# FFN 2's down-projection in seven products instead of eight

## The chip, the cores and the metric

The kernel runs on one core of one Trainium2 chip. The metric is the device time of one execution in microseconds (us). Before the change the median of three runs is 3400.17 us (3399.27 to 3403.31).

## What is computed

One inference step of a decoder layer over 1056 tokens (1024 of a prompt, 32 of samples), D_MODEL 1024, D_FF 2816. Only the last part matters here:

```python
def swiglu(x, w_in, w_out):
    gate, up = jnp.split(x @ w_in, 2, axis=-1)
    return (jax.nn.silu(gate) * up) @ w_out

y = h + 0.5 * rmsnorm(swiglu(rmsnorm(h, ffn2_pre), ffn2_w_in, ffn2_w_out), ffn2_post)
```

All values are float32. The kernel splits each operand of a matmul into a high and a low half (a cast to fp32r, and the difference to the value) and adds three matmuls: high by high, high by low, low by high. A tile of weights or of hidden values therefore costs a load, a cast on ScalarE and a subtraction on VectorE before TensorE can use it.

## The kernel before

Both FFNs are built by `ffn_units`; FFN 2 is called from `outputs_ffn`. Each engine has an in-order queue, written out by hand, and semaphores say when an operation may start. `sync`, `scalar`, `vector`, `gpsimd` and `tensor` are the queues of SP (which issues all loads and stores here), ScalarE, VectorE, POOL and TensorE; each calls `during(h, k)` at its step, by which `outputs_ffn` puts its own work (norms, turned rows, stores) between the steps.

The up-projection ends with hidden row tiles t = 0 to 21 of 128 features by 1056 tokens. It already uses seven products in place of eight (`product`, L2887), with weight sums on POOL (L2829 to L2834). Each finished row tile is stored to DRAM as `d_hid` (`store_h`, L2510).

The down-projection (`out_step`, L2897) multiplies `w_out` (22 tiles of 128 features by 1024) with the hidden values. Tokens are in chunks (`SPANS`): 0 to 383, 384 to 767, and the last 288. For each chunk there are two passes, one for each half of the output features: h = 0 to 5. In a pass, at every k of 22, one unit of weights u = 22 h + k (128 x 512) meets hidden tile k, in 4 output blocks by 3 matmuls: 12 matmuls. Sums stay in four PSUM banks, and the passes alternate between banks 0 to 3 and 4 to 7.

A unit is loaded to one of eight raw slots (`load_unit`, L2560), cast (`unit_high`, L2568) to one of four slots, and its low half made (`unit_low`, L2572). The cast of u + 3 waits until TensorE is through with u - 1. Hidden tiles come back from `d_hid` one at a time (`load_hid`, L2584; `hid_high`, L2594; `hid_low`, L2600) through a ring of four. POOL has only sums of squares here (`sum_pool`, L2981). After a chunk's two passes come `square` (L2966), `copy_out` (L2974, L2972), the mean (`sum_y`), `root_y`, `norm` (L3010), the residual sum (L3981), transposes of rows (L4120), copies of these (L3849) and stores; the last chunk has its residual transposed early (L4141, copied by L3853) and ends the kernel with L4145, L4151 and L4006.

Of the kernel before, what the change touches and what calls it, by code (L numbers as in the profile page):

```python
# [2348 lines left out]
def ffn_units(nc, m, sem, w_in, w_out, d_hid, first_hi, first_lo, x, t_val, t_hi, t_lo, pair_mem, hid_hi, hid_lo, gb, rstd, pre, spans, acc, staged):  # L2349
# [18 lines left out]
    e.y_normed, e.h_resid = sem("y_normed"), sem("h_resid")  # L2368
    win = w_in.rearrange("o (f p) n -> p (o f) n", p=P)
# [232 lines left out]

    EARLY = {2: range(0, 3), 3: range(3, 6), 4: range(6, 8), 5: range(8, 10)}
    BEFORE = 10

    def sync(sp, before_odd, during):
        load_pair(sp, 2)
# [38 lines left out]
    def scalar(act, t_free, during):  # L2646
# [6 lines left out]
        for t in range(2, FT):  # L2653
# [8 lines left out]
            for i in range(7):  # L2662
                if s + 6 + i < N1:
                    pair_high(act, s + 6 + i)
                elif i in (3, 4, 5):
                    unit_high(act, i - 3)
                if t == FT - 1 and i in EARLY:
                    for n in EARLY[i]:
                        hid_high(act, n)
                if i in (4, 6):  # L2670
                    a = (i - 4) // 2
                    act.wait_ge(e.gate_done, 6 + 2 * (t - 2) + a + 1)
                    nc.scalar.activation(silu[:, halves(a)], silu[:, halves(a)], ACT.Silu).then_inc(e.silu_done, 1)
        for h in range(6):
# [50 lines left out]
    def vector(dve, scale_in, between, during):  # L2725
# [14 lines left out]
        for t in range(2, FT):  # L2740
# [5 lines left out]
            def next_low(i):  # L2746
                if s + 6 + i < N1:
                    pair_low(dve, s + 6 + i)
                elif i in (3, 4, 5):
                    unit_low(dve, i - 3)  # L2750
                if t == FT - 1 and i in EARLY:
# [46 lines left out]
        pair_h(dve, FT - 1, 1)  # L2798
        for h in range(6):
# [17 lines left out]
    def gpsimd(pool, x_dead):  # L2817
        t_differences(pool)
        x_dead()
        for t in range(2, FT):  # L2820
# [14 lines left out]
            if t == 2:  # L2835
                t_low_pool(pool)

# [63 lines left out]
    def tensor(pe, during, bank_free):  # L2901
# [10 lines left out]
        for t in range(2, FT):  # L2912
            for i in range(7):
                product(pe, t, i)
        for h in range(6):
# [27 lines left out]
    def result(j):  # L2943
        c, o = divmod(j, KT)
        lo, hi = spans[c]
        return m.ps[:, o, 0:hi - lo], acc[:, o, 0:hi - lo]
# [10 lines left out]
    def square(act, j):  # L2957
        c, o = divmod(j, KT)
        act.wait_ge(e.out_mm, output_done(j))
# [6 lines left out]
        nc.scalar.activation(ring(c, o) if o else total(c), result(j)[0], ACT.Square).then_inc(e.y_squared, 1)  # L2966
# [9 lines left out]
    def sum_pool(pool, c):  # L2976
        for o in range(1, 8 if c < 2 else 4):
# [5 lines left out]
    def sum_y(pe, c, bank):  # L2983
        lo, hi = spans[c]
        mean = m.cst[:, C_MEAN:C_MEAN + P]
        if c < 2:
            pe.wait_ge(e.y_copied, KT * c + bank + 1)
# [17 lines left out]
    def norm(dve, c, f, post):  # L3005
        y = result(KT * c + f)[1]
        if f == 0:
            dve.wait_ge(e.y_rooted, c + 1)
            dve.wait_ge(e.y_copied, KT * c + KT)
# [6 lines left out]
    e.total, e.ring, e.last_gain = total, ring, None  # L3016
# [518 lines left out]
def outputs_ffn(nc, m, keep, w_a, w_b, w_o, gates, ob_dram, d_resid, d_hid, w_in, w_out, y_prompt, y_sample):  # L3535
# [8 lines left out]
    with ExitStack() as ctx:  # L3544
# [32 lines left out]
        pair_mem, acc = m.pair_mem, m.acc_chunk  # L3577
# [9 lines left out]
        def staged_hid(c, k):  # L3587
# [5 lines left out]
                      SPANS, acc, staged_hid)  # L3593
# [11 lines left out]
        def pair(i):  # L3605
            return (6, 4, 6, 6, 4, 6, 2, 4, 6)[i]
# [6 lines left out]
        def row_out(i):  # L3613
            n = P if i < TT else NS
            return row_of(i)[0:n, :].rearrange("p (b f) -> p b f", b=2), m.ps[0:n, pair(i):pair(i) + 2, :]
# [23 lines left out]
        def _(sp):  # L3639
# [55 lines left out]
            def res_load(c):  # L3695
                lo, hi = SPANS[c]
                if c == 0:
                    sp.wait_ge(e.y_copied, 1)
# [15 lines left out]
            def during(h, k):  # L3714
                if h in (1, 3) and k == 6:
                    res_load(h // 2)
                elif h == 3 and k == 8:
                    sp.dma_start(res_last, d_resid[:, :, 6 * P:T]).then_inc(res_in_last, 16)
                elif h in (3, 5) and k in (0, 1, 2):
                    store_row(3 * (h // 2 - 1) + k)  # L3720
# [7 lines left out]
        def _(act):  # L3728
# [117 lines left out]
            def row(i):  # L3846
                dst, src = row_out(i)
                act.wait_ge(turned, i + 1)
                nc.scalar.copy(dst, src).then_inc(row_act, 1)  # L3849

            def res_row(t):
                act.wait_ge(res_mm, t + 1)
                nc.scalar.copy(row_of(6 + t).rearrange("p (b f) -> p b f", b=2), m.ps[:, 6:8, :]).then_inc(res_moved, 1)  # L3853

            def during(h, k):
                if h == 4 and k in (8, 10, 12):
                    res_row((k - 8) // 2)
                if h in (2, 4):
                    if k == 6:
                        e.root_y(act, h // 2 - 1, 4)  # L3860
                    elif k in (18, 19):
                        row(3 * (h // 2 - 1) + k - 18)
                    elif k == 21:
                        row(3 * (h // 2 - 1) + 2)
# [447 lines left out]
```

## Time and profile before

| | us |
|---|---|
| median of three runs | 3400.17 |
| the profiled execution's span | 3400.1 |
| TensorE busy | 3305.8 (97%) |
| VectorE busy | 1871.2 (55%) |
| ScalarE busy | 1456.3 (43%) |
| POOL busy | 700.0 (21%) |
| HBM read and written | 309.92 MB, 75.57 MB |

The span is that of the one execution that was profiled. A busy share is an average over stages with different limits; the change touches about the last 290 us, so the rows below are mostly of that stretch. The granted TensorE clock is given as a share of full speed: 1.00 is 2.4 GHz.

### The profile page before, as it was taken

Reading aid. Unit: us, or ns where it says so; the run is one execution under the profiler, and the core shown is the slowest. Engines: PE = TensorE matmul, PEld = TensorE weight load, DVE = VectorE, ACT = ScalarE, POOL = GpSimd, SP = SyncE. Lnnn points to the kernel's source line nnn. Section 1 sums busy time; section 2 is a strip of 40 time slices with the busy share of each in tenths; the row PEclk is TensorE's granted clock in tenths of the full one; section 3 lists DMA queues with packets and bytes.
Section 4 is the critical chain, followed back from the end, with each engine's and each line's share of the span. In section 5 each row is a group of like instructions: output and inputs, shape, how many; then the busy total and the mean of one; then the engine's idle time right before and its main releaser. Section 6 shows DMA issues by size and latency. Waiting matters only on the chain. (4 is left out here: it accounts for less than half of the span.)

```text
span 3400.1 us, 70872 instructions
## 1 busy us (share of the span) xinstructions
PE 3305.8 (97%) x28190; PEld 3137.6 (92%) x28190; DVE 1871.2 (55%) x3334; ACT 1456.3 (43%) x3056; POOL 700.0 (21%) x651
## 2 busy tenths in 40 slices
PE   7999999998999999999999999999999899999999
PEld 7999999997888888877899999998999899999998
DVE  6655565764555555554455555554441855556555
ACT  5222234555555455443344444444323722223444
POOL 3323310112222222100022222222001332221000
PEclk9999999999999999999999999999999999999999
DMA  4222237742222222379511122224532322224664
GB/s 167 76 79 79 87 109 230 221 135 81 70 70 70 71 70 70 109 254 369 188 47 56 58 59 59 59 59 136 165 88 70 123 86 76 76 76 151 200 207 132
DMA packets 353606, 390.03 MB, mean 115 GB/s; under 512 B 22792, under 2 KB 259416, under 8 KB 353134
## 3 DMA queue, kind: packets, MB, share of 16 engines
q1 hardware_dynamic: 343126, 352.18, 33.1%
q0 software_dynamic: 10080, 33.05, 2.7%
q8 instruction: 228, 3.74, 0.5%
q14 instruction: 88, 0.72, 0.1%
q10 hardware_dynamic: 84, 0.35, 0.0%
HBM read 309.92 MB, written 75.57 MB: 113 GB/s over the span
## 5 line engine op out<-in xcount | busy, mean ns | idle before, releaser
L673 PE MATMUL ps<-p_hi,w_hi 128*128 128x352 f32 x912 | 305.6, 335 | 1.8 <-PEq L123 1.4
L673 PE MATMUL ps<-p_hi,w_lo 128*128 128x352 f32 x912 | 294.5, 323 | 0.0
L673 PE MATMUL ps<-p_lo,w_hi 128*128 128x352 f32 x912 | 294.0, 322 | 0.0
L2062 PE MATMUL ps<-p_hi,w_hi 128*128 128x352 f32 x840 | 291.0, 346 | 2.7 <-PEq L123 1.4
L2062 PE MATMUL ps<-p_hi,w_lo 128*128 128x352 f32 x840 | 277.2, 330 | 0.0
L2062 PE MATMUL ps<-p_lo,w_hi 128*128 128x352 f32 x840 | 277.2, 330 | 0.0
L673 PEld LDWEIGHTS ps<-p_hi,w_hi 128*128 128x128 f32 x912 | 173.1, 190 | 4.2 <-issue 2.7
L2897 PE MATMUL ps<-op_hid_hi,w_hi 128*128 128x384 f32 (+1 forms) x528 | 171.5, 325 | 3.7 <-DVE w_lo L2572 2.0
L673 PEld LDWEIGHTS ps<-p_lo,w_hi 128*128 128x128 f32 x912 | 173.2, 190 | 0.0
L2897 PE MATMUL ps<-f_hid_hi,w_hi 128*128 128x352 f32 x528 | 171.5, 325 | 1.6 <-DVE w_lo L2572 1.6
L673 PEld LDWEIGHTS ps<-p_hi,w_lo 128*128 128x128 f32 x912 | 172.2, 189 | 0.0
L2897 PE MATMUL ps<-f_hid_lo,w_hi 128*128 128x352 f32 x528 | 170.0, 322 | 0.0
L2897 PE MATMUL ps<-f_hid_hi,w_lo 128*128 128x352 f32 x528 | 169.9, 322 | 0.0
L2897 PE MATMUL ps<-op_hid_hi,w_lo 128*128 128x384 f32 (+1 forms) x528 | 169.6, 321 | 0.0
L2897 PE MATMUL ps<-op_hid_lo,w_hi 128*128 128x384 f32 (+1 forms) x528 | 169.6, 321 | 0.0
L2062 PEld LDWEIGHTS ps<-p_hi,w_hi 128*128 128x128 f32 x840 | 160.5, 191 | 8.2 <-issue 3.1
L2062 PEld LDWEIGHTS ps<-p_lo,w_hi 128*128 128x128 f32 x840 | 160.9, 192 | 0.2
L2062 PEld LDWEIGHTS ps<-p_hi,w_lo 128*128 128x128 f32 x840 | 160.5, 191 | 0.0
L2572 DVE TENSOR_TENSOR w_lo<-w_raw,w_hi 128x512 fp32r<-128x512 f32 x136 | 100.5, 746 | 83.2 <-ACT w_hi L2568 82.8
L414 ACT ACTIVATE at_prob<-ps,at_nmax 128x256 f32<-128x256 f32 (+7 forms) x128 | 94.2, 737 | 82.4 <-DVE at_nmax L520 80.7
L2568 ACT CAST w_hi<-w_raw 128x512 fp32r<-128x512 f32 x136 | 83.8, 620 | 100.5 <-PE ps L2897 100.1
L347 ACT ACTIVATE at_rotx<-ps 32x352 f32<-32x352 f32 x192 | 87.4, 455 | 88.6 <-DVE at_cosx L468 54.7
(707 smaller groups left out, 10374.4 us busy)
## 6 DMA issues: line engine op xcount, KB each, us to landing
w_raw<-in_ffn_w_out_dram SPq DMA_DIRECT2D x136, 256.0 KB, 3.4
w_raw<-in_w_in_dram SPq DMA_DIRECT2D x67, 512.0 KB, 4.2
sa_v<-in_cache_v_dram SPq DMA_DIRECT2D x120, 256.0 KB, 6.7
w_raw<-in_ffn_w_in_dram SPq DMA_DIRECT2D x48, 512.0 KB, 5.1
sa_k<-in_cache_k_dram SPq DMA_DIRECT2D x72, 256.0 KB, 5.5
f_s<-in_ffn_w_out_dram SPq DMA_DIRECT2D x64, 256.0 KB, 3.5
pair_s<-in_ffn_w_out_dram SPq DMA_DIRECT2D x64, 256.0 KB, 3.2
d_hid<-f_gb SPq DMA_DIRECT2D x44, 264.0 KB, 2.1
```

Source lines behind the costliest of these rows:

```text
L347: ins = nc.scalar.mul(dst, src, HD ** -0.5 if kind == "q" else 1.0)
L414: nc.scalar.activation(pr[:, i % 2, a, 0:(i + 1) * P], m.ps[:, 2 + 2 * a:4 + 2 * a, :].rearrange("p b k -> p (b k)")[:, 0:(i + 1) * P], AC ...
L673: mm = nc.tensor.matmul(m.ps[:, bank, 0:CH], a[:, k, w], b[:, f, cols(c)], start=(f == 0 and i == 0), stop=(f == KT - 1 and i == 2))
L2062: mm = nc.tensor.matmul(m.ps[:, (k + c) % 2, 0:CH], a[:, k, f * P:(f + 1) * P], x[:, f, cols(c)], start=(j == 0), stop=(j == len(terms) - 1))
L2568: nc.scalar.copy(unit_slot(u, False), unit_raw(u)).then_inc(e.out_hi, 1)
L2572: nc.vector.tensor_tensor(unit_slot(u, True), unit_raw(u), unit_slot(u, False).bitcast(F32), ALU.subtract).then_inc(e.out_lo, 1)
L2897: mm = nc.tensor.matmul(m.ps[:, bank, 0:hi - lo], unit_slot(u, low_part)[:, o * P:(o + 1) * P], y[:, k, 0:hi - lo], start=(k == 0 and n == ...
```

## The change

For chunks 0 and 1 together (768 tokens) the product of `w_out` and the hidden values is cut in quadrants: hidden features in two halves of 11 tiles, tokens in two chunks of 384 (W3), output features in two halves of 512. Seven products p = 0 to 6 of 11 steps each take the place of four passes of 22. Every product needs an operand of hidden values that is a quadrant or a sum of two (`x_sum`, in parts of 4, 3 and 4 tiles; VectorE makes parts 0 and 2, POOL part 1, for products 3 to 6), then a cast (`x_high`) and a low half (`x_low`). Five of the products (1, 2, 3, 4, 6) use the sum or difference of two weight tiles: two raw loads and an addition on POOL (`w_sum`) ahead of the cast. After each product its four banks are copied or added to blocks of `acc` (`read_act`, `read_dve`), which grows from one chunk to two. The quarters of hidden values are loaded tile by tile (`load_quad`), but those of product 0 in three larger loads (`load_first_parts`). The last chunk keeps plain products, as steps h = 7 and 8 of `during`; its low halves move to POOL (`rest_low`). FFN 1 keeps its own code.

```diff
@@ def ffn_units
+    KH = FT // 2
+    W3 = 3 * P
+    GROUPS = ((0, 4), (4, 7), (7, KH))
+    SOURCES = (((1, 1),), ((0, 1), (1, 1)), ((0, 0), (1, 0)), ((0, 0), (1, 1)), ((1, 0), (1, 1)), ((0, 0),), ((0, 1), (0, 0)))
+    def load_raw(sp, r):
...
+        elif RAWS[r - 8][1] == 1:
+            sp.wait_ge(e.w_sum, SUM_OF[RAWS[r - 8][0]])
+        else:
+            sp.wait_ge(e.out_lo, RAWS[r - 8][0] + 1)
...
+    def load_first_parts(sp, g):
+        lo, hi = GROUPS[g]
+        if g == 0:
+            sp.wait_ge(e.up_mm, 12 + N1 - 6)
+        else:
+            sp.wait_ge(e.hid_lo, part_count(0, g - 1))
...
+    def w_sum(pool, v):
+        r = RAW_OF[v]
+        raw_there(pool, r)
+        raw_there(pool, r + 1)
+        op = ALU.subtract if v // KH in MINUS else ALU.add
+        nc.gpsimd.tensor_tensor(unit_raw(r), unit_raw(r), unit_raw(r + 1), op).then_inc(e.w_sum, 1)
...
+    def w_high(act, v):
+        if v in SUM_OF:
+            act.wait_ge(e.w_sum, SUM_OF[v])
+        else:
+            raw_there(act, RAW_OF[v])
...
+            act.wait_ge(e.out_mm, used(v - 4))
+        nc.scalar.copy(unit_slot(v, False), unit_raw(RAW_OF[v])).then_inc(e.out_hi, 1)
...
+    def quad_sync(sp, before_odd, during):
...
+        for v in range(NQ):
+            p, k = divmod(v, KH)
+            raws(v + 6 if p else v + 8)
+            if v == 0:
+                load_first_parts(sp, 2)
+            elif v <= 6:
+                for n in range(2 * v - 2, min(2 * v, KH)):
+                    load_quad(sp, 0, 0, n)
+            elif v <= 17:
+                load_quad(sp, 1, 1, v - 7)
+            elif v <= 28:
+                load_quad(sp, 1, 0, v - 18)
+            elif 33 <= v <= 43:
+                load_quad(sp, 0, 1, v - 33)
+            elif v == 62:
+                for n in range(4):
+                    load_rest(sp, n)
+            elif p == 6 and k >= 3:
+                load_rest(sp, k + 1)
+            during(p, k)
...
+    def quad_scalar(act, during):
+        for v in range(NQ):
+            p, k = divmod(v, KH)
+            w_high(act, v + 3)
+            if p == 0:
+                if k == 0:
+                    x_high(act, 0, 1)
+                elif k == 4:
+                    x_high(act, 0, 2)
+                elif k in (8, 9):
+                    x_high(act, 1, k - 8)
+            else:
+                if k == 0:
+                    read_act(act, p - 1)
...
+    def quad_vector(dve, during):
+        for v in range(NQ):
+            p, k = divmod(v, KH)
+            w_low(dve, v + 3)
+            if p == 0:
+                if k == 0:
+                    x_low(dve, 0, 1)
+                elif k == 4:
+                    x_sum(dve, nc.vector, 0, 2, e.x_sum)
+                elif k == 5:
+                    x_low(dve, 0, 2)
+                elif k in (9, 10):
+                    x_low(dve, 1, k - 9)
...
+                if k == 0:
+                    read_dve(dve, p - 1, False)
+                elif k == 1 and summed:
+                    x_sum(dve, nc.vector, p + 1, 0, e.x_sum)
+                elif k == 2:
+                    read_dve(dve, p - 1, True)
+                elif k == 3 and p < 6:
+                    x_low(dve, p + 1, 0)
+                elif k == 4 and summed:
+                    x_sum(dve, nc.vector, p + 1, 2, e.x_sum)
+                elif k == 5 and p < 6:
+                    x_low(dve, p + 1, 1)
+                elif k == 7 and p < 6:
+                    x_low(dve, p + 1, 2)
+            during(p, k)
...
+    def quad_gpsimd(pool, during):
+        for p in (1, 2, 3, 4):
+            for k in range(KH):
+                w_sum(pool, KH * p + k)
+                if k == 3 and p + 1 in X_SUM_POOL:
+                    x_sum(pool, nc.gpsimd, p + 1, 1, e.x_sum_pool)
+            during(p)
+        x_sum(pool, nc.gpsimd, 6, 1, e.x_sum_pool)
+        during(5)
+        for k in range(KH):
+            w_sum(pool, KH * 6 + k)
+            if k >= 6:
+                rest_low(pool, k - 6)
+        sum_pool(pool, 1, 1, 4)
...
+    def quad_tensor(pe, during, bank_free):
+        for p in range(7):
+            for k in range(KH):
+                v = KH * p + k
+                during(p, k)
+                pe.wait_ge(e.out_lo, v + 1)
+                for g in range(3):
+                    if k == GROUPS[g][0]:
+                        pe.wait_ge(e.hid_lo, part_count(p, g))
...
```

## Rows read from the trace of the kernel before

**Rows 1.** The page: busy us of each engine, share of the span, instructions.
```profile
PE 3305.8 (97%) x28190; PEld 3137.6 (92%) x28190; DVE 1871.2 (55%) x3334; ACT 1456.3 (43%) x3056; POOL 700.0 (21%) x651
```
**Rows 2.** The chain of waits, 2900 to 3400: start us, us, what.
```profile
3223.89 24.99 PE ps L2897 x144
...
3330.82 9.48 PE ps L2897 x72
```
**Rows 3.** Who TensorE waited for, 3090 to 3400; and the stall's row.
```profile
PE ps L2897 <- DVE w_lo L2572: 2.0, 2, 1.7
PE ps L2897 <- ACT plain L3849: 1.7, 2, 1.0
...
3127.28 0.44 PE L2897 MATMUL ps<-op_hid_hi,w_hi 128*128 128x384 f32 x1 [1.70 <-DVE w_lo L2572]
```
**Rows 4.** Groups by line and shape, 3000 to 3400: busy us, mean ns, idle before.
```profile
L2572 DVE TENSOR_TENSOR w_lo<-w_raw,w_hi 128x512 fp32r<-128x512 f32 x68 | 49.1, 728 | 49.8 <-ACT w_hi L2568 49.4
...
L2568 ACT CAST w_hi<-w_raw 128x512 fp32r<-128x512 f32 x68 | 42.0, 621 | 58.8 <-PE ps L2897 58.6
...
L2594 ACT CAST op_hid_hi<-plain 128x384 fp32r<-128x384 f32 x44 | 22.5, 511 | 17.4 <-DMA plain<-d_hid 16.8
...
L3981 DVE TENSOR_TENSOR acc_chunk<-acc_chunk,plain 128x1536 f32<-128x1536 f32 x4 | 7.0, 1752 | 0.0
...
L3849 ACT COPY plain<-ps 128x1024 f32<-128x1024 f32 x6 | 6.0, 1007 | 0.0
```
**Rows 5.** Timelines, 3100 to 3128: SP's issues, and TensorE's turn to the down-projection.
```profile
3100.30 4.39 SPq L2510 DMA_DIRECT2D d_hid<-op_gb  x2
3104.74 1.88 SPq L2560 DMA_DIRECT2D pair_s<-in_ffn_w_out_dram  x4
...
3119.03 0.28 PE L2887 MATMUL ps<-p_hi,pair_ex_lo 128*128 128x264 f32 x1
3119.15 0.34 PE L2897 MATMUL ps<-op_hid_hi,w_hi 128*128 128x384 f32 x1
```
**Rows 6.** Landings in 3222 to 3262 and 3265 to 3300; windows, ending in DMA share, GB/s.
```profile
DMA to landing us min/median/max: 2.5/2.8/4.1
...
q1 hardware_dynamic: 7244, 10.41, 91.1%
...
pair_s<-in_ffn_w_out_dram SPq DMA_DIRECT2D x10, 256.0 KB, 5.2
w_raw<-in_ffn_w_out_dram SPq DMA_DIRECT2D x8, 256.0 KB, 4.1
...
3275.00:3285.00 10.00, 10.00 (x60) 10.00 (x59) 4.99 (x10) 4.54 (x9) 0.00 (x0) 1.00 1.04 353
...
1575.00:1610.00 35.00, 35.00 (x510) 29.55 (x510) 15.11 (x42) 11.46 (x27) 1.60 (x3) 1.00 1.04 381
```
**Rows 7.** Timeline, 3062 to 3070, VectorE and POOL: start us, us.
```profile
3062.78 0.70 DVE L2723 TENSOR_TENSOR op_gb<-op_gb 128x528 f32<-128x528 f32 x1
3062.95 1.69 POOL L2829 TENSOR_TENSOR pair_s<-w_raw 128x512 f32<-128x512 f32 x1 [14.01 <-DVE p_lo L2531]
...
3066.37 1.30 POOL L2832 TENSOR_TENSOR pair_s<-w_raw 128x512 f32<-128x512 f32 x1
...
3067.48 0.73 DVE L2531 TENSOR_TENSOR p_lo<-pair_s,p_hi 128x512 fp32r<-128x512 f32 x1
3067.61 1.75 POOL L2834 TENSOR_TENSOR pair_s<-w_raw,pair_s 128x512 f32<-128x512 f32 x1
```
**Rows 8.** Timeline, 3218 to 3221, VectorE and POOL one by one.
```profile
3218.01 1.28 POOL L2981 TENSOR_TENSOR op_gb<-op_gb 128x384 f32<-128x384 f32 x1
...
3218.33 1.50 DVE L2572 TENSOR_TENSOR w_lo<-w_raw,w_hi 128x512 fp32r<-128x512 f32 x1
...
3219.43 1.28 POOL L2981 TENSOR_TENSOR op_gb<-op_gb 128x384 f32<-128x384 f32 x1
```
**Rows 9.** The DMA view, 1530 to 1610: KB each, median us to landing.
```profile
sa_v<-in_cache_v_dram SPq DMA_DIRECT2D x56, 256.0 KB, 7.1
```

More of the change, by code:

```diff
@@ new lines, in add_block, with read_dve @@
+    def add_block(q, i, j):
+        for half in range(2):
+            y = block_of(i, j, half)
+            if q == 1:
+                nc.vector.wait_ge(e.read_act, READ_ACT[0] + half + 1)
+            nc.vector.tensor_tensor(y, pass_bank(q, half), y, ALU.add).then_inc(e.read_dve, 1)
+    def read_dve(dve, q, second):
+        if not second:
+            dve.wait_ge(e.out_mm, KH * (q + 1))
+            wait(dve, e.read_dve, READ_DVE[q - 1])
+        if q == 1:
+            if not second:
+                add_block(q, 1, 0)
+        elif q == 2:
+            if not second:
+                for half in range(2):
+                    y = block_of(0, 0, half)
+                    dve.wait_ge(e.read_act, READ_ACT[1] + half + 1)
+                    nc.vector.scalar_tensor_tensor(out=y, in0=pass_bank(q, half), scalar=-1.0, in1=y, op0=ALU.mult, op1=ALU.add).then_inc(e.read_dve, 1)
+        elif q == 3:
+            add_block(q, *((1, 1) if second else (0, 0)))
+        elif q == 4:
+            if not second:
+                add_block(q, 0, 0)
+        elif q == 5:
+            add_block(q, *((1, 1) if second else (0, 1)))
+        elif not second:
+            add_block(q, 1, 1)
@@ new lines, in quad_gpsimd @@
+    def quad_gpsimd(pool, during):
[12 more added lines that the diff above has]
+        sum_pool(pool, 1, 1, 4)
+        for n in range(5, 11):
+            rest_low(pool, n)
+        sum_pool(pool, 1, 4, 6)
+        for n in range(11, 13):
+            rest_low(pool, n)
+        sum_pool(pool, 1, 6, 8)
+        for n in range(13, FT):
+            rest_low(pool, n)
@@ L2974, in copy_out, with sum_pool @@
             nc.vector.tensor_copy(result(j)[1], result(j)[0]).then_inc(e.y_copied, 1)
-    def sum_pool(pool, c):
-        for o in range(1, 8 if c < 2 else 4):
+    def sum_pool(pool, c, first=1, end=None):
+        for o in range(first, end or (8 if c < 2 else 4)):
             pool.wait_ge(e.y_squared, KT * c + o + 1)
@@ L3576, in outputs_ffn @@
         gb = place(ctx, "gb", [P, 2, T])
-        pair_mem, acc = m.pair_mem, m.acc_chunk
+        pair_mem, acc = m.pair_mem, [m.acc_chunk[:, c, :, :] for c in range(2)]
         def h_squares(c, a):
@@ L4026, in _, with during @@
             pool.wait_ge(summed, 4)
[L4027 to L4029 removed]
+            def during(h):
+                if h == 4:
+                    e.sum_pool(pool, 0, 1, 4)
+                elif h == 5:
+                    e.sum_pool(pool, 0, 4, KT)
+            e.gpsimd(pool, lambda: pool.wait_ge(spilled, 48), during)
+            e.sum_pool(pool, 2)
         @block.tensor
```

475 lines of the change are left out of this document (400 added, 75 removed).

## The prediction

> **What bounds the kernel now.** I read the page first: TensorE is busy for 97% of 3400.1 us, VectorE 55%, POOL 21% [rows 1]. The whole change lies after the last up-projection, so the second view is the groups by line of the stretch 3000 to 3400, and the third the chain of waits there. The chain runs through L2897, the down-projection, almost without a break: 144 of its 384-column matmuls take 24.99 us, 0.1735 us each, and 72 of its 288-column ones 9.48 us, 0.1317 us each [rows 2]. (A matmul's own row says 0.34 us [rows 5], because neighbours overlap; the chain's pitch is the price.) TensorE waits in this stretch for little: 2.0 us for a low half of a weight tile, 1.7 us for copies of turned rows [rows 3]. So TensorE bounds, and the question is whether fewer matmuls are still fed. Per weight tile of 12 matmuls (2.08 us) ScalarE now works 0.62 us (L2568) and VectorE 0.73 us (L2572), and POOL nothing [rows 4].
>
> **What is removed.** Chunks 0 and 1 now take 4 passes of 22 tiles of 12 matmuls, 1056. Seven products of 11 tiles take 924. 132 fewer at 0.1735 us: **-22.9 us**, all on the path. Chunk 2 keeps its 528. The norms, squares, turned rows and stores are moved between steps, not added; they cost nothing while they lie under matmuls as they do now. The stall of 1.7 us for a low half, at 3125.6 [rows 3], came from VectorE working through separate small hidden tiles; in the new order the same low half is ready at about 3124.7: **-1.7 us**.
>
> **Start of product 0.** Its operand, the difference of two hidden quarters, is made in three parts. I follow the queues from the rows. The up-projection ends at 3119.2 (the last L2887 row, then the first L2897 row) [rows 5]. Part 0 (two loads, 1.57 MB) is issued at 3104.7, where SP is done with a store [rows 5]. A load of that size takes 6.4 us: 2.1 us fixed (a 256 KB load lands in 2.8 us in a quiet stretch, of which 0.7 us is transfer) and 4.3 us at 353 to 381 GB/s [rows 6]. So it is there at 3111.3, its sum (1536 elements, 1.75 us as L3981), high half (1.5 us) and low half (1.7 us) [rows 4] are done at 3116.4, and product 0 starts in time. SP asks for part 1 only when part 0's low half is made (3116.4), and for part 2 when part 1's is (3126.0, as VectorE has seven more operations of the up-projection in front). Part 2 lands at 3132.6; sum, cast, an interposed weight tile and difference end at 3138.9. TensorE needs it at its eighth tile, 3119.3 + 7 x 2.08 = 3133.9: **+5.0 us**. The load could be 2 us quicker or slower, so 3 to 7.
>
> The Trainium skill, DMA: Bandwidth & Descriptors, "Two cost components", fits a load as 2.0 us and bytes over 436 GB/s. By that estimate part 2 lands in 5.6 us and the stall is 4.2 us; rows here never show over 381 GB/s in a stretch, so they decide.
>
> ScalarE waits for part 2 in order, so SP's loads behind it are late too: the last tile of quarter (0,0) is issued at 3140.8, lands at 3144.2, and product 1's first low half is ready at 3148.7 where TensorE would come at 3147.2: **+1.5 us** (0 to 4).
>
> **The port.** Products 1, 2, 3, 4 and 6 need a sum of two weight tiles on POOL before every cast. A 128x512 add there takes 1.29 us alone but 1.69 to 1.75 us in most rows. The reason is in the timeline [rows 7]: the add that begins at 3067.61 ends at 3069.36, 1.15 us after VectorE's p_lo ended (3068.21); the one at 3062.95 ends at 3064.64, 1.16 us after L2723 (3063.48). Only the one at 3066.37, beside which VectorE reads ps, takes 1.30. The reverse holds as well [rows 8]: a w_lo starts at 3218.33, stays until POOL's add ends at 3219.29, and ends 0.55 us later; the next add then waits for it and ends 0.87 us later. So a VectorE operation with two inputs in SBUF and a POOL add exclude each other, and each holds the port for its turn: w_lo 0.55 us, 384-element POOL add 0.87 us (2.27 ns an element), 512-element add 1.16 us, VectorE 1.05 ns an element. PSUM readers (the new reads of the products, VectorE) are free.
>
> The port's work in a product, against TensorE's 11 x 2.08 = 22.9 us:
> Products 2, 3 and 4 each: 11 weight sums 12.8, 11 w_lo 6.1, three low parts of 4224 elements in all 4.5, two VectorE sums (3072 elements) 3.2, one POOL sum (1152 elements) 2.6; sum 29.2 us. Product 1: 12.8 + 6.1 + 4.5 + 1.6 (a left-over part) = 25.0. Together 112.6 us. When product 1 starts, five weight sums and three low halves are done (7.4 us), and the last tile must be ready 2.1 us before the end: 112.6 - 7.4 + 2.1 = 107.3, against 4 x 22.9 = 91.6: **+16 us**. Products 5 and 6 together: VectorE 12.1 + 4.5 + 3.2, norms and residual 7; POOL 12.8 weight sums, sums of squares and the x sum 8.7, five low halves of chunk 2 of 3.3; 51.6 against 45.8: **+6 us**. The last chunk's first pass has about 36 us of port work in 34.8 us, mostly ahead of need; I take nothing. Bounds: that VectorE and POOL interleave better than their turns, down to 0 if buffers hid it all; up to +32 if each loses another 10% of port time waiting for loads and casts. I take the sum of the turns, which rows 7 and 8 show without a gap.
>
> The Trainium skill, SBUF — State Buffer, "Who interferes with whom", states this lock, for the whole instruction of either side. The rows agree that one blocks the other, but give 1.16 us for what lasts 1.29 alone. With 1.29 the 55 sums would add 7.2 us, 3411 us in all; that lies inside the case below.
>
> **Other covers.** SP issues three loads a tile, 0.47 us each by the four in 1.88 us [rows 5], so 1.4 of 2.08 us: hidden. A tile paced by SP alone would still be no slower than now. The ScalarE reads of products 0 to 2 (eight of 768 columns, about 0.8 us by L3849's 1.01 us for 1024 [rows 4]) sit in ScalarE's queue ahead of casts that have three tiles, 6 us, in hand: 0; uncovered they would cost 6.6 us. The waits of SP on rest_lo, in product 6, queue weight loads behind them; the loads are needed over 4 us later: 0, at most 3.
>
> **Sum**, against the profiled span 3400.1, which is also the median of 3400.17: 3400.1 - 22.9 - 1.7 + 5.0 + 1.5 + 16 + 6 = 3404.0; waits in order seldom cost less than their sum, so I say **3405**.
>
> **Rivals.** *A, the forecast: the port binds*, 3396 to 3413, chance 0.50. *B, the port is hidden*: TensorE's ring of four tiles and POOL's ring of four sums take up the turns, and only the start is paid: 3400.1 - 24.6 + 6.5 = 3382, up to 3396 with half of the port's cost. For it: VectorE is idle for 49.8 us in front of one of the two w_lo groups now [rows 4], and POOL is all but unused. Against it: 29.2 us of exclusive turns don't fit in 22.9 whatever the rings. Chance 0.30. *C, slower: the ring of raw weight slots binds.* Eight slots now hold four pairs in place of eight tiles. A pair's circle is landing, blocked sum 1.7, cast 0.6, blocked low half 1.3 and 0.4 of hand-overs: 4.0 us and the landing. Four tiles of TensorE are 8.3 us, so it decides from a landing of 4.3 us, and above the port's pace (2.65 us a tile) from 6.6 us. Quiet loads land in 2.8 us; where the DMA share is 0.91 they take 4.1 and 5.2 us, and in the attention part 7.1 us [rows 6, 9]. Products 1 to 3 ask for 22 x 0.262 + 11 x 0.197 = 7.9 MB in 22.9 us, 346 GB/s, which is about the share at which those rows stand. With 7.1 us a tile takes 2.78 us: 55 tiles x 0.70 - 6.8 in hand = 31.7 in place of 22, so 3414, and with residual loads in the way up to 3425. Against it: a kernel slowed by the port asks for less. Chance 0.20.
>
> **How the numbers follow.** B gives 0.27 faster and 0.03 same; A, around 3405 with same reaching to 3407, 0.30 same and 0.20 slower; C 0.20 slower. Same is within 0.2% (3393.4 to 3407.0), about what a measurement of this kernel can tell from no change. The range 3385 to 3423 leaves out 0.1 on each side; A's own is 3396 to 3413.
>
> **What would show it.** Step 1: L2897's successor has 924 + 528 matmuls at 0.174 and 0.132 us. Start: one TensorE stall of 3 to 7 us at the eighth tile, released by the low part of product 0. Port: the POOL weight sums at 1.7 us or more against 1.29 alone, w_lo's mean well over 0.73 us, and TensorE stalls on w_lo spread over products 2 to 4, 16 us in sum; B shows fewer than 5. C shows them too, but with w_raw landings over 6 us and POOL idle before its sums for the DMA. Wrong would be: stalls elsewhere (POOL's sums of squares at the last chunk, SP behind rest loads), or PSUM reads on VectorE that turn out not to be free.

## The result and the profile after

| | before | after |
|---|---|---|
| median of the runs, us | 3401.74 (3399.27 to 3404.34) | 3438.26 (3437.02 to 3441.92) |
| the profiled execution's span, us | 3400.1 | 3435.4 |

The ratio is 1.0112, with a 95% interval of 1.0098 to 1.0127: the medians are 36.5 us apart. The forecast was 3405, its range ended at 3423. The likeliest sign was right, the size was missed by 33 us; no rival reached that far either (the slowest, C, ended at 3425).

The page of the kernel after: span and busy us of each engine. Against [rows 1] TensorE has 132 matmuls fewer but is busy for only 8.6 us less, VectorE for 68 more, POOL for 129 more.

```profile
span 3435.4 us, 70668 instructions
...
PE 3297.2 (96%) x28058; PEld 3121.8 (91%) x28058; DVE 1939.1 (56%) x3289; ACT 1463.8 (43%) x3030; POOL 828.8 (24%) x732
```

Who TensorE waited for, 3090 to 3436: us in total, times, longest. L3030 is the products' matmul, L3037 the last chunk's, L2770 the weights' low half, L2742 the operand's, L4638 the turned rows, which wait for the residual sum (L4494), L4661 the turned residual, which waits for its row copy (L4354). [rows 3] showed 3.7 us of this kind.

```profile
PE ps L3030 <- DVE w_lo L2770: 25.8, 18, 4.9
PE ps L4638 <- DVE acc_chunk L4494: 9.0, 2, 7.6
PE ps L3030 <- DVE op_hid_lo L2742: 7.0, 1, 7.0
PE ps L4661 <- ACT plain L4354: 4.4, 2, 3.7
```

Groups by line and shape, 3119 to 3436: busy us, mean ns, idle before. L2749 is the weight sum on POOL (17 + 16 + 11 + 11 of them; two of the four groups are shown).

```profile
L2770 DVE TENSOR_TENSOR w_lo<-pair_s,w_hi 128x512 fp32r<-128x512 f32 x61 | 58.9, 973 | 48.1 <-ACT w_hi L2766 47.8
L2770 DVE TENSOR_TENSOR w_lo<-w_raw,w_hi 128x512 fp32r<-128x512 f32 x57 | 57.1, 1005 | 36.1 <-ACT w_hi L2766 35.4
...
L2749 POOL TENSOR_TENSOR w_raw<-w_raw 128x512 f32<-128x512 f32 x17 | 28.4, 1672 | 16.4 <-DMA w_raw<-in_ffn_w_out_dram 16.4
L2749 POOL TENSOR_TENSOR pair_s<-pair_s 128x512 f32<-128x512 f32 x16 | 25.5, 1596 | 20.7 <-DMA pair_s<-in_ffn_w_out_dram 20.7
```

The low half of a weight tile takes 973 to 1005 ns where [rows 4] had 728, the sum 1.60 to 1.70 us where one alone takes 1.30 [rows 7]. That is the port at work, but it is not yet a price.

For the price I cut the stage at the first matmul of every product and pass (all times in us, from the starts of the matmul rows; the forecast is the working's, spread over the products):

| | ideal or before | forecast | after | over forecast |
|---|---|---|---|---|
| product 0 | 22.9 | 27.9 | 33.1 | 5.2 |
| products 1 to 4 | 91.6 | 108.8 | 29.5 + 31.0 + 29.9 + 36.2 = 126.6 | 17.8 |
| products 5 and 6 | 45.8 | 51.6, and 4.9 of transposes and small waits | 24.1 + 37.7 = 61.8 | 5.3 |
| last chunk, first pass | 42.2 | 42.2 | 48.7 | 6.5 |
| last chunk, second pass | 49.4 | 49.4 | 50.3 | 0.9 |
| sum | | 284.8 | 320.5 | 35.7 |

The pieces are cut at starts, so a wait for the first tile of product 1 lies in product 0; the forecast has its +1.5 us under products 1 to 4. The 4.9 us are what the first four passes of before (189.4 us) take beyond 1056 x 0.1735 = 183.2 and the stall of 1.7 that was to go, with the roundings. The whole stage took 280.9 before. That the profiled spans differ by 35.3 and not by 39.6 is because work ahead of the stage, which the change doesn't touch, ended 4.3 us earlier in the profiled execution of after. Over the profiled executions of all versions the start of this stage varies by 8 us (3114.3 to 3122.4). The 95% intervals of the medians are 4 to 9 us to either side. So small differences below are read from the pieces, of which there is one profile each, and a median decides alone only where it moves by more than its interval.

### The profile page after: what moved, and what is told of

Read it like the earlier page. It is cut to its first block and busy times, and to the rows that moved or that the text cites. A ratio compares the mean times of both kernels' runs of the same rounds, so it can differ in the third digit from the quotient of the medians.

```text
span 3435.4 us, 70668 instructions
## 1 busy us (share of the span) xinstructions
PE 3297.2 (96%) x28058; PEld 3121.8 (91%) x28058; DVE 1939.1 (56%) x3289; ACT 1463.8 (43%) x3030; POOL 828.8 (24%) x732
## 5 line engine op out<-in xcount | busy, mean ns | idle before, releaser
L3030 PE MATMUL ps<-op_hid_hi,w_hi 128*128 128x384 f32 x308 | 110.2, 358 | 33.8 <-DVE w_lo L2770 25.8
L517 DVE TENSOR_TENSOR ps<-ps,cst 128x128 f32<-128x128 f32 x128 | 37.6, 293 | 135.3 <-PE ps L740 132.5
L3366 PE MATMUL ps<-p_hi,w_hi 128*128 128x264 f32 x384 | 108.9, 284 | 2.8 <-DVE w_lo L2537 2.8
L3366 PE MATMUL ps<-p_lo,w_hi 128*128 128x264 f32 x384 | 109.1, 284 | 0.0
L3366 PE MATMUL ps<-p_hi,w_lo 128*128 128x264 f32 x384 | 109.1, 284 | 0.0
```

Of the source, the lines that this page charges most:

```text
L517: nc.vector.tensor_tensor(s[:, i * P:(i + 1) * P], s[:, i * P:(i + 1) * P], m.cst[:, C_CAUS:C_CAUS + P], ALU.add).then_inc(masked, 1)
L3030: mm = nc.tensor.matmul(m.ps[:, 4 * (p % 2) + o, 0:W3], unit_slot(v, low_part)[:, o * P:(o + 1) * P], y[:, x, :], start=(k == 0 and n == 0 ...
L3366: mm = nc.tensor.matmul(m.ps[:, bank + n, 0:HB], w_slot(s, lo)[:, w], y, start=(i < 4 and f == 0 and q == 0), stop=((i >= 4 or i == 1) and ...
```

## Experiments

Every kernel is the changed one with the edit shown. "Product" times are those of the table above.

**1. Is it POOL's sums?** The sum covers 8 of 512 columns; every wait and hand-over stays.

```diff
-        nc.gpsimd.tensor_tensor(unit_raw(r), unit_raw(r), unit_raw(r + 1), op).then_inc(e.w_sum, 1)
+        nc.gpsimd.tensor_tensor(unit_raw(r)[:, 0:8], unit_raw(r)[:, 0:8], unit_raw(r + 1)[:, 0:8], op).then_inc(e.w_sum, 1)
```

> Leaves out most of the weight sums: POOL adds only 8 of the 512 columns of each pair, so the rest of the sum is left out and the result is not the reference's. All waits and both loads stay. Port theory (VectorE and POOL exclude each other when both read SBUF): the 55 sums of 1.16 us leave the port, w_lo goes back from 0.99 to about 0.73 us, TensorE's stalls in products 1 to 4 and 6 (about 37 us with the low clock behind them) go but for those of the hidden parts: 3438 becomes 3403 to 3412. Ring theory (landing of the two raw tiles): the circle of a raw slot is 1.6 us shorter of 8.7, so it gains too, 3410 to 3425. This run gives the whole price of the sums; the next one splits it.

Measured: 3410.21, ratio 1.0032 (1.0021 to 1.0043). Groups by line and waits of TensorE, same stretch:

```profile
L2770 DVE TENSOR_TENSOR w_lo<-pair_s,w_hi 128x512 fp32r<-128x512 f32 x61 | 47.9, 792 | 51.6 <-ACT w_hi L2766 51.3
...
PE ps L3030 <- DVE w_lo L2770: 8.4, 4, 3.3
PE ps L3030 <- DVE op_hid_lo L2742: 7.0, 1, 7.0
PE ps L4638 <- DVE acc_chunk L4494: 3.6, 2, 2.3
```

The low half is back at 792 ns, the waits for it fall from 25.8 to 8.4 us, and products 2 and 3 take 22.99 and 23.13 us: the ideal 22.9. So the sums cost 28 us, and the price of 132 matmuls is confirmed. But 10.6 us above before remain with the sums all but gone, where rival B said 3382: another 28 us that are not the weight sums. (POOL still makes its part of the operands, the sums of squares and the last chunk's low halves here, so the port is lighter and not free.)

**2. POOL's time, or the port?** Two fills of 504 columns take the sum's place; a fill reads nothing.

```diff
+        nc.gpsimd.memset(unit_raw(r)[:, 8:512], 0.5)
+        nc.gpsimd.memset(unit_raw(r + 1)[:, 8:512], 0.5)
         nc.gpsimd.tensor_tensor(unit_raw(r)[:, 0:8], unit_raw(r)[:, 0:8], unit_raw(r + 1)[:, 0:8], op).then_inc(e.w_sum, 1)
```

> Replaces each weight sum by two POOL fills of 504 columns (about 0.5 us each) and a sum of 8 columns, so POOL is as long busy as with the sum alone (1.2 us) but reads almost nothing from SBUF. The weights of five products are replaced by a constant. Port theory: within 5 us of the tiny-sum kernel, w_lo about 0.73 to 0.8 us. Theory that POOL's own queue or the added latency of its step in the slot's circle is what costs: within 5 us of 3438 instead.

Measured: 3413.29, ratio 1.0036 (1.0022 to 1.0050). Groups by line:

```profile
L2772 DVE TENSOR_TENSOR w_lo<-pair_s,w_hi 128x512 fp32r<-128x512 f32 x61 | 49.1, 811 | 55.5 <-ACT w_hi L2768 55.5
...
L2749 POOL MEMSET w_raw<- 128x504 f32 x28 | 14.6, 520 | 72.9 <-DMA pair_s<-in_ffn_w_out_dram 57.3 <-DMA w_raw<-in_ffn_w_out_dram 15.5
...
L2751 POOL TENSOR_TENSOR w_raw<-w_raw 128x8 f32<-128x8 f32 x17 | 9.1, 536 | 0.0
```

POOL now works 2 x 0.52 + 0.5 = 1.5 us a tile, more than the 1.3 us of an undisturbed sum, and yet the low half takes 811 ns and 25 of the 28 us stay gone. It is what POOL reads beside VectorE, not how long it works. The Trainium skill, SBUF — State Buffer, "Who interferes with whom", says that a two-input VectorE instruction contends with a GpSimd instruction that reads SBUF and not with one that only writes it; the 811 ns against 792 and 973 agree.

**3. Landings or the raw ring (rival C)?** The second weight tile of each sum loads 8 of 512 columns.

```diff
+        w = 8 if n == 1 else 512
+        sp.dma_start(unit_raw(r)[:, 0:w], wout[:, k, half * 512:half * 512 + w]).then_inc(e.out_full[r % 8], 16)
```

> The second raw tile of each pair is loaded in 8 of its 512 columns only, the sum still runs over 512 (so most of the second addend is an old tile, and the sums are wrong). DMA bytes of products 1 to 4 and 6 fall by almost half, landings should fall from 4.2 to 4.9 to about 3 us. Ring theory: the stalls of products 1 to 4 go, 3410 to 3420. Port theory: the turns stay, w_lo stays near 0.99 us and the time falls by no more than 8 us, 3430 to 3438.

Measured: 3438.89, ratio 1.0107 (1.0087 to 1.0127). The landings did get quicker: in 3168 to 3240 the medians of full weight tiles fell from 4.3 and 3.9 us to 2.8 and 2.9. Product 1 came down from 29.5 to 24.0 and product 4 from 36.2 to 34.6; products 0, 2 and 6 rose by 1.1 to 1.2 us each, and the total stayed. The low halves are as slow as before (910 and 1055 ns), and products 2 and 3 take 32.1 and 30.2. Rival C falls as the cause of the 28 us: with half of the bytes of every sum gone, the port still sets the pace. Product 1 is another matter, and waits for a load (below).

**4. The sums on VectorE**, at the place where POOL did them (w_sum for v + 4 after the low half of v + 3).

```diff
-        nc.gpsimd.tensor_tensor(unit_raw(r), unit_raw(r), unit_raw(r + 1), op).then_inc(e.w_sum, 1)
+        nc.vector.tensor_tensor(unit_raw(r), unit_raw(r), unit_raw(r + 1), op).then_inc(e.w_sum, 1)
```

> Computes everything. The weight sums move from POOL to VectorE, one step earlier than they are needed. Port theory: a sum then holds the port 0.55 in place of 1.16 us, 22.5 in place of 29.2 us a product, and nothing waits for its turn; VectorE itself has 24 to 26 us of work a product against 22.9, so 3415 to 3425. Theory that VectorE's time as such is the limit and the port is not: 30 us more VectorE work make it slower than 3438.

Measured: 3429.53, ratio 1.0080 (1.006 to 1.010). A sum costs 0.68 to 0.76 us there in place of 1.16 us of port, the low half is at 0.79 us. That is 8.7 us faster, the direction of the port theory, but short of its 3415 to 3425. Products 2 and 3 take 29.1 and 27.0, of which VectorE is busy for 26.9 and 23.3: its own queue now holds more than 22.9 us.

**5. The start.** The second part of product 0's operand gets slots of its own, so that the third is loaded as soon as the first part's low half is made and not the second's; its last tile goes separately. The loads of quarters (0,0) and (1,1) get a wait for the second part's low half. (Part of the edit.)

```diff
+        f = HALF if g == 1 else 0
...
-            sp.wait_ge(e.hid_lo, part_count(0, g - 1))
+            sp.wait_ge(e.hid_lo, part_count(0, 0))
...
+                sp.wait_ge(e.hid_lo, part_count(0, 1))
```

> Computes everything. Of product 0's operand, part 1 gets a place of its own, and part 2 (except its last tile) is loaded as soon as part 0's low half is made, its last tile in a small load behind the last store. Theory of the late part 2: its landing no longer ends the wait, product 0 falls from 33.1 to 23 to 26 us, no 7.3 us stall and no low clock behind it; 3438 becomes 3428 to 3432. Rival (VectorE's queue, not the load, is late at the eighth tile): product 0 stays above 30 us. Products 2 to 4 unchanged by both.

Measured: 3437.82, ratio 1.0109 (1.0089 to 1.0129). Product 0 went from 33.1 to 29.5 (expected: 23 to 26), and the median did not move. Product 6 gave 1.5 of the 3.6 us back, and the stage is 2.2 us shorter in this execution. Waits of TensorE:

```profile
PE ps L3040 <- DVE w_lo L2779: 26.0, 19, 4.9
...
PE ps L3040 <- issue: 3.7, 1, 3.7
...
PE ps L3040 <- DVE op_hid_lo L2751: 2.4, 1, 2.4
```

The stall on the operand fell from 7.0 to 2.4. A new one of 3.7 at the end of product 0 has no releaser in this view, but the rows around it show its cause:

```profile
3144.09 1.48 ACT L2747 CAST op_hid_hi<-plain 128x1536 fp32r<-128x1536 f32 x1 [3.67 <-DMA plain<-d_hid]
3147.83 1.74 DVE L2751 TENSOR_TENSOR op_hid_lo<-plain,op_hid_hi 128x1536 fp32r<-128x1536 f32 x1
...
3149.68 0.66 PE L3040 MATMUL ps<-op_hid_hi,w_hi 128*128 128x384 f32 x1 [3.72 <-issue]
```

ScalarE waits for the last tile of quarter (0,0), casts product 1's first part, and TensorE starts product 1 0.1 us after VectorE ends that part's low half (3149.57). The same 0.1 us stands in the kernel after (3147.85 and 3147.95, a gap of 1.3 us between matmul starts) and in experiments 7, 10 and 11. It is the prediction's +1.5 us, the load of quarter (0,0): with the first stall shortened, TensorE reaches the end of product 0 6.4 us sooner after the stage's start, the low half is made only 3.6 us sooner, and the wait shows.

**6. The quarters.** Quarter (1,1) is asked for over steps 7 to 13 in place of 7 to 17, quarter (0,1) four steps earlier.

```diff
-            elif v <= 17:
-                load_quad(sp, 1, 1, v - 7)
+            elif v <= 13:
+                for n in ((0, 1), (2,), (3, 4), (5,), (6, 7), (8,), (9, 10))[v - 7]:
+                    load_quad(sp, 1, 1, n)
...
-            elif 33 <= v <= 43:
-                load_quad(sp, 0, 1, v - 33)
+            elif v <= 39:
+                load_quad(sp, 0, 1, v - 29)
```

> Computes everything. The quarters (1,1) and (0,1) of hidden values are loaded four steps earlier. Theory: the 5 us stall in product 1 (ScalarE's cast in order behind the last tile of (1,1)) and the one of 5 us in product 4 (POOL's sum in order behind the last tile of (0,1), with the weight sums behind it) go: products 1 and 4 from 29.5 and 36.2 to 25 and 31, 3438 becomes 3427 to 3431. Rival: by the port alone those products take 25.0 and 29.2 us, and more backlog takes the place of the waits, so less than 5 us are gained.

Measured: 3435.07, ratio 1.0095 (1.007 to 1.012). Product 1 fell from 29.5 to 26.8, product 4 from 36.2 to 32.0, which shows that both waits were for these tiles; products 2 and 3 gave 1.5 of it back (32.0 and 30.4). This execution's stage is 6.6 us shorter (314.0). The median moved by 3, less than its interval, and short of the expected 3427 to 3431.

**7. Edits 4, 5 and 6 together.**

> Computes everything. The three changes together: sums on VectorE, the split start, the earlier quarters. If the causes are separate, the gains of 9, 8 and 9 us add up: 3438 - 26 = 3412, with products 2 to 4 at 25 to 28 us each. If VectorE's own time binds (24 to 26 us of work a product), about 3415 to 3418.

Measured: 3423.35, ratio 1.0069 (1.0050 to 1.0088). Products 30.4, 24.6, 29.5, 30.2, 30.5, 23.7, 35.0. That is 15 us faster than the changed kernel, but outside both ranges: products 2 to 4 stay at 30, with VectorE busy for 27 to 28 us in each. Against experiment 4 the two edits of order give 6 us, in the median as in the stage.

**8. As 7, with every second sum on POOL again.**

```diff
+        engine = nc.vector if v % 2 else nc.gpsimd
+        engine.tensor_tensor(unit_raw(r), unit_raw(r), unit_raw(r + 1), op).then_inc(e.w_sum_dve if v % 2 else e.w_sum, 1)
```

> Computes everything. As the last one, but only every second weight sum on VectorE, the others on POOL. The port then has 25.8 us of work in products 2 to 4 and VectorE itself 19 to 21 us. Port theory: products 2 to 4 at 26 to 28 us, so about equal to the last one, 3408 to 3418. Theory that VectorE's in-order time binds once the sums are there: 5 to 10 us faster than the last one.

Measured: 3428.27, ratio 1.0088 (1.0071 to 1.0105). Both theories missed. Halfway is 5 us above all on VectorE; the two intervals overlap, but the profiled stage is 4.4 us longer as well (308.6 and 304.3), in products 2 and 4: 32.5 and 33.7 in place of 29.5 and 30.5.

**9. Edits 1, 5 and 6 together:** the orders mended while the port is free.

> Leaves out most of the weight sums (8 of 512 columns are added), and has the split start and the earlier quarters. Those two gained nothing and 3 us with the sums in place. Theory of the backlog: they gained nothing because the port's work, 29 us a product, only moved the wait; with the sums gone from the port they gain what their waits cost, 3 to 4 us at the start and 7 to 9 us in products 1 and 4: 3410 becomes 3396 to 3400. Rival (the waits' repair is worthless for another reason, such as late low halves at the start): 3406 to 3410.

Measured: 3399.50, ratio 0.9995 (0.9982 to 1.0008). By the medians the two edits gave 0 and 3 us, each alone, beside the full sums, and 11 together beside sums of 8 columns, as expected. The pieces don't bear the theory out: there they shorten the stage by 2.2 and 6.6 us beside the full sums, and by 7.3 (289.0 to 281.7) beside the small ones, where the gain sits in the same products 0, 1 and 4. And the two were never run together beside POOL's full sums. So it isn't shown that a wait mended while the port is behind is only handed to it.

**10. Edit 7 and the end of the stage:** residual loads of chunk 1 from step 6 of the last chunk's pass, norms and residual sums of chunk 0 a step earlier, turned rows a step later.

```diff
-                elif h == 7 and k == 0:
+                elif h == 7 and k == 6:
...
-                pairs = {(5, 9): (0, 0), (5, 10): (0, 1), (6, 1): (0, 2), (6, 3): (0, 3), (7, 10): (1, 0), (7, 11): (1, 1), (7, 12): (1, 2), (7, 13): (1, 3)}
+                pairs = {(5, 8): (0, 0), (5, 9): (0, 1), (5, 10): (0, 2), (6, 1): (0, 3), (7, 10): (1, 0), (7, 11): (1, 1), (7, 12): (1, 2), (7, 13): (1, 3)}
...
-                if h == 6 and k in (7, 8, 9):
+                if h == 6 and k in (8, 9, 10):
```

> Computes everything. The kernel with all sums on VectorE, the split start and the earlier quarters, and besides: chunk 1's residual is loaded at step 6 of the last chunk's first pass and not at step 0, the norms and residual of chunk 0 come one step earlier on VectorE, and its rows are turned one step later. Theory that the first pass of the last chunk is late by loads (raw tiles behind a 1.5 MB residual and three stores): that pass falls from 49.7 to 43 to 45 us, and product 6 from 35.0 to 29 to 31 us: 3423 becomes 3411 to 3415. Rival (POOL's in-order low halves and sums of squares make it late): the pass stays at 49 us.

Measured: 3417.97, ratio 1.0041 (1.0024 to 1.0058), the best that computes the whole result. Product 6 fell from 35.0 to 29.3, as expected; the last chunk's pass did not (50.9, from 49.7). For the pass the rival's figure held (POOL's low halves and sums of squares in order).

**11. Edits 1, 5, 6 and the tail of 10.**

> Leaves out most of the weight sums like the tiny-sum kernels, with all repairs: split start, earlier quarters, later residual load and later rows. It is what the seven products would give if the sums of weights cost nothing. All 11.2 us of the start beyond 22.9 and the 6.5 of the last chunk should go except some 5 us: 3387 to 3393, so below the kernel before. If it stays above 3397, something other than the sums and the four places named takes the gain.

Measured: 3397.72, ratio 0.9991 (0.9977 to 1.0006). This is above the expected 3387 to 3393, and by 0.7 above the 3397 from which something else had to be at work. Product 6 is at 25.5 and products 1 to 3 at 23.0, 22.9 and 24.2. Of the 15.7 us above rival B's 3382, 10.5 lie in the last chunk's first pass (52.7 against 42.2) and 4.9 in product 4 (27.8). The same pass took 49.1 in experiment 9: the later residual load and rows made it 3.5 us longer. The residual now lands after 10.8 us, and SP, with weight loads behind, waits 7.9 us for row copies that it is to store (4.4 in experiment 9). The timeline of ScalarE at 3300 to 3328 shows how the pass goes late; in brackets its wait for a landing:

```profile
3307.66 0.62 ACT L2775 CAST w_hi<-pair_s 128x512 fp32r<-128x512 f32 x1 [2.92 <-DMA pair_s<-in_ffn_w_out_dram]
...
3319.68 0.62 ACT L2775 CAST w_hi<-w_raw 128x512 fp32r<-128x512 f32 x1 [3.08 <-DMA w_raw<-in_ffn_w_out_dram]
```

**12. Is it the transfers in that pass?** The changed kernel, with the weight loads of this pass cut to 8 of 512 columns.

```diff
+        w = 8 if NQ <= v < NQ + FT else 512
+        sp.dma_start(unit_raw(r)[:, 0:w], wout[:, k, half * 512:half * 512 + w]).then_inc(e.out_full[r % 8], 16)
```

> The changed kernel, but the weight loads of the last chunk's first pass fetch only 8 of 512 columns (the output of the last chunk is left wrong; nothing else is changed, every cast, low half and matmul stays). It asks what makes that pass last 48.7 us in place of 42.2: TensorE waits 4.4 us there for a row copy on ScalarE, and the DMA queue is 88% busy with weights, hidden tiles, the residual and row stores at once, weights landing in 5 to 6 us. Theory T (transfers): with 5.7 MB of 8.5 MB gone, landings fall under 4 us, ScalarE no longer waits for weights ahead of the row copy, the 4.4 us and its clock loss go, and the pass lasts 42 to 44 us; product 6, in which the loads of the first tiles are issued, loses up to 2 us; median 3430 to 3434. Rival O (order): the row copy is late because of what stands before it in the queues (the residual sum on VectorE after product 6, which ended late), whatever the transfers take; then the pass keeps 47 to 50 us and the median stays at 3436 to 3440.

Measured: 3437.64, ratio 1.0106 (1.0089 to 1.0123). The pass went from 48.7 to 45.2: between the two theories. The first fence is the DMA view of after, 3337 to 3365 (count, KB each, median us to landing), the second that of this kernel, 3339 to 3367, with TensorE's waits.

```profile
pair_s<-in_ffn_w_out_dram SPq DMA_DIRECT2D x8, 256.0 KB, 6.2
...
q1 hardware_dynamic: 5072, 8.55, 88.5%
```

```profile
pair_s<-in_ffn_w_out_dram SPq DMA_DIRECT2D x8, 4.0 KB, 3.7
...
plain<-d_resid SPq DMA_DIRECT2D x1, 1536.0 KB, 8.0
...
PE ps L4662 <- ACT plain L4355: 2.3, 2, 2.1
```

So 3.5 of the 6.5 us go with the bytes of these weights: TensorE waits 2.1 us less for the row copy, and the 3.4 us at the lower clock are gone. Of the other 3, 1.4 are a wait of the turned rows for VectorE's residual sum that every changed version has and before has not; 2.3 are the rest of the wait for the row copy, where before had 0.8. That rest is no pure matter of late issue. Two rows of SP's timeline in this kernel, the landing times of its weight loads issued at 3336 to 3356, and a row of ScalarE's:

```profile
3342.51 0.53 SPq L4196 DMA_DIRECT2D plain<-d_resid  x1
3343.08 0.66 SPq L2664 DMA_DIRECT2D w_raw<-in_ffn_w_out_dram  x1
...
DMA to landing us min/median/max: 1.9/3.8/7.6
...
3350.69 0.62 ACT L2767 CAST w_hi<-w_raw 128x512 fp32r<-128x512 f32 x1 [1.94 <-DMA w_raw<-in_ffn_w_out_dram]
```

A weight load of 4 KB that is issued right behind the residual of 1.5 MB lands after 7.6 us, and ScalarE's longest wait is for it. The chain of waits of the kernel after shows the order in front of such loads:

```profile
3340.34 1.14 POOL op_gb L3474
...
3341.61 1.28 POOL op_gb L3474
3342.89 0.78 POOL op_hid_lo L2790
3343.68 0.32 SPq L2781
3344.05 0.68 SPq L4199
3344.77 0.86 SPq L2663
3345.68 0.71 SPq L2781
3346.43 0.46 SPq L4199
3346.93 7.21 DMA pair_s<-in_ffn_w_out_dram
...
3361.45 0.92 ACT plain L4354
```

POOL's low half of a hidden tile stands behind two sums of squares (L3474), SP's load of the next hidden tile (L2781) waits for it, and a row store (L4199) and the weight load (L2663) stand behind that one. The weight load then takes 7.2 us among the residual and the stores. Before, the same hidden tiles were all issued by 3302.6, 6 us before the pass began, the residual by 3276.6, and the first of the row stores at 3347.0, 38 us into the pass. How the rest of the 3 us divides between the residual's transfer and POOL's order was not tried. The median did not follow (the stage began 7.6 us later in this execution than in that of after, and was 4.8 us shorter), so the split rests on the pieces alone.

## Why the prediction was wrong

The 33 us are two misses. With the weight sums all but gone the kernel takes 3410 and not B's 3382; this is 28 us. The sums then add 28 and not the 22 of the forecast. The step that failed: the working followed two waits for loads through the in-order queues (+5.0 and +1.5 us) and put every other cover but the port at 0. The runs show TensorE stopped behind quarter (1,1) in product 1, quarter (0,1) in product 4, the turned rows in product 6 and the loads of the last chunk's first pass, and slowed by the clock with most of these stops; and the 5.3 us "in hand" of the port term didn't exist. The stage of experiment 1 is 26 us above B's: 4.9 in product 0, 3.5 in product 1, 7.4 in product 4, 2.5 in products 5 and 6, 6.7 in the last chunk's first pass, the rest under 1.

**Right.** 924 + 528 matmuls, 22.9 us fewer: products 2 and 3 of experiment 1 take the ideal time. The stall of 1.7 us that was to go is gone. The mechanism of the port: the lock, its release by moving the sums, and the pace of products 2 and 3 (29.2 forecast, 31.0 and 29.9 measured; VectorE is busy, its blocked time included, for 29.5 and 29.0 of them). The +1.5 us for quarter (0,0), 1.3 measured. Rival C was no cause here. PSUM readers on VectorE cost nothing visible (L2820, 768 columns: 0.94 us, and 0.95 without POOL's sums).

**The "in hand" of the port term.** I took port turns as work to be divided over four products, with 7.4 us done before and 2.1 needed early: 5.3 us saved. Four weight sums were done when product 1 began, but at the starts of products 2, 3 and 4 there were two of the coming product's each time (13, 24 and 35 in all), so these drew nothing from a stock. It was lost in product 1, where POOL once waited 6.3 us for a load. Against the turns themselves product 1 is 4.5 over, products 2 and 3 are 2.5, product 4 is 7.0; with the 5.3 that is all of the 19.3 us over 107.3. Product 4 shows how it comes about. POOL one by one, 3237 to 3252:

```profile
3241.41 1.28 POOL L2749 TENSOR_TENSOR w_raw<-w_raw,pair_s 128x512 f32<-128x512 f32 x1 [2.30 <-DMA pair_s<-in_ffn_w_out_dram]
3245.72 2.63 POOL L2722 TENSOR_TENSOR plain<-plain 128x1152 f32<-128x1152 f32 x1 [3.03 <-DMA plain<-d_hid]
3248.31 1.26 POOL L2749 TENSOR_TENSOR pair_s<-pair_s 128x512 f32<-128x512 f32 x1
```

POOL's part of the operand waits 3.0 us for quarter (0,1) and takes 2.6; the weight sums stand behind it, and TensorE stops for 4.9 us at 3246.5. This wait, queued ahead of weight sums, is a step that my working lacked; experiment 6 shows it to be worth 4 us in this product.

**Product 0: 5.2 over.** The stall was forecast at the eighth tile and is there, with 7.0 us in place of 5.0. The chain of waits gives the term:

```profile
3121.82 0.37 SPq L2676
...
3122.24 7.98 DMA plain<-d_hid
...
3130.24 1.77 DVE plain L2722
...
3134.75 1.67 DVE op_hid_lo L2742
```

The load took 8.0 us where I said 6.4 (the first part's took 6.3). The window of it shows the engines shared with weight and quarter loads, at 309 GB/s and not the 353 to 381 of [rows 6]:

```profile
3122.00:3130.00 8.00, 7.57 (x44) 7.25 (x42) 2.29 (x4) 0.62 (x1) 0.00 (x0) 1.00 0.92 309
```

By the Trainium skill, DMA: Bandwidth & Descriptors, "Two cost components", 5.6 us is the estimate for a load of this size; the trace differs, and decides. My remark that rows never pass 381 GB/s holds for the windows that I asked for, and not for single slices of the DMA view (405 in 1275 to 1400). The rest of the 5.2 us is the clock (2.0, below) and the wait of 1.3 us for quarter (0,0) at the end of the product, which the forecast has under product 1.

**Product 1: 6.6 over its 22.9.** The +1.5 for quarter (0,0) came before it, as shown. Inside the product there is a second wait: ScalarE's cast of product 2's first part stands ahead of weight casts, and waits for the last tile of quarter (1,1). The row, 3163 to 3173:

```profile
3169.03 1.47 ACT L2738 CAST op_hid_hi<-plain 128x1536 fp32r<-128x1536 f32 x1 [6.39 <-DMA plain<-d_hid]
```

TensorE's stall is 5.2 us. I had followed one quarter through the queues and not the other three.

**Terms put at nothing.** Two of them failed. The turned rows were to cost nothing under the matmuls; in product 6 they wait 7.6 us for the residual sum, which VectorE reaches late: with the weight sums all but gone (experiment 1) they wait 2.3. Experiment 10 moves steps by one and gets 5.7 us back. And the last chunk's first pass, taken at nothing because its port work is ahead of need, is 6.5 over. The change keeps the slots of the last chunk's operand in use by products 5 and 6, so its hidden tiles are loaded in the pass itself, together with the residual, the row stores and the weights (experiment 12). I followed the waits on rest_lo for the loads they delay in product 6 and put 0, at most 3; I didn't carry them into the pass. Yet I had named it as a sign of being wrong, "POOL's sums of squares at the last chunk, SP behind rest loads", and that is what the chain shows. [rows 6] had the warning too: landings of 5.2 us at a share of 0.91.

**The clock, not priced at all.** During a long stall the granted clock falls to the lower of its two levels, and it stays there when TensorE goes on. Windows of after around the first stall (3129.6 to 3136.6; the clock fell at 3133.9): us, PE, PEld, VectorE, ScalarE, POOL busy (instructions), then granted clock, DMA share, GB/s.

```profile
3133.00:3137.00 4.00, 0.44 (x1) 0.47 (x2) 2.94 (x3) 2.06 (x4) 1.85 (x1) 0.61 1.07 378
3137.00:3140.00 3.00, 3.00 (x11) 3.00 (x11) 2.78 (x2) 0.00 (x0) 2.35 (x3) 0.50 0.84 284
3140.00:3143.00 3.00, 3.00 (x17) 3.00 (x16) 0.69 (x1) 0.62 (x1) 1.16 (x1) 0.88 0.64 177
3143.00:3146.00 3.00, 3.00 (x20) 3.00 (x18) 0.51 (x1) 2.54 (x3) 1.29 (x1) 1.00 0.76 232
```

The counts are of matmuls that touch the window. At 0.50 (1.2 GHz) 384-column matmuls start 0.32 us apart, at 1.00 (2.4 GHz) 0.17. In the stage the clock stood at 0.50 for 34 us in six stretches, stalls included, with stalls of 7.3, 5.2, 2.4, 4.9, 7.9 and 4.0 us (from matmul start to matmul start, some 0.3 us longer than the waits above); after one other of 2.4 us, one of 2.1 and the many of 1.5 or less it did not fall. Before, there was one such stretch, at the end, which both kernels have. Added up, matmul starts that are 0.25 to 0.5 us apart cost 13 us over the normal pitch (before: 1.6), 9.4 of them inside the six stretches. Not all of the 9.4 us are lost, since part lies where the port would have made TensorE wait anyway; product 0, where nothing binds after the stall, pays 2.0 of them in full. So a stall that is counted by its own length is undersized by some tenths of it.

**What stays open.** How the last pass's other 3 us divide; why experiment 5's local gain didn't reach the median; whether mended waits are worth less beside the busy port; why half of the sums on VectorE is no better than all. In the last pass only the places of the residual's load and the rows were tried, together, and it got longer (by 1.2 us in experiment 10, by 3.5 in 11). No version tried beats the kernel before; experiment 11, which leaves most of the sums out, only draws level. That bounds what a free pre-sum of the weights could bring with the rest as it is.

## What to carry to other kernels

When a change saves time on the engine that bounds, ask first what it asks of in-order queues: list every operation that waits for a load, and what is queued behind it, for all of the loads and not for the one nearest the start. A sum on POOL beside a VectorE that reads two operands in SBUF costs the port and is not free because POOL is idle. Price a stall of TensorE of 4 us and more above its length. When one wait is mended, look for the next one in line: the shorter stall in product 0 laid bare 3.7 us of waiting for quarter (0,0). And judge a repair by the pieces of the stage as well as by the median: the same two edits looked like 3 us and 11 us by medians, and like 9 and 7 by the stage.

## What was not expected of the hardware

The clock's fall in the middle of a stage in which TensorE is busy for 265 of 320.6 us, with single stalls (0.50 for 3.4 to 10.2 us with each of 4.0 us and more, and with one of two of 2.4). That POOL's fills, 1.0 us of them a tile, left VectorE's low half at 811 ns, against 973 to 1005 beside sums of 1.3 us. That a load of 4 KB behind one of 1.5 MB took 7.6 us to land. And that VectorE adds two 128x512 tiles in 0.68 to 0.76 us where POOL takes 1.60 to 1.70 in its company, and yet 55 sums more on it leave products 2 to 4 at 27 to 33 us.
